# Stick-breaking sums as head and rest products in fp32r, with softplus moved between weight pieces, and differential masks over two blocks

## The reference, cut to what matters

```
z = einsum('bqhd,bkhd->bhqk', qb, k) * scale
log_1m_beta = where(strict, log_sigmoid(-z), 0.0)
suffix = cumsum(log_1m_beta, axis=3, reverse=True) - log_1m_beta
a = where(strict, exp(log_sigmoid(z) + suffix), 0.0)
o = einsum('bhqk,bkhd->bqhd', a, v)
```

## Time and profile before

| | |
|---|---|
| median of 3 runs | 1457.71 us (1454.75 to 1459.5) |
| the profiled execution's own time | 1457.98 us |
| its span, first to last instruction | 1456.3 us |
| PE busy | 1394.3 us (96%), 6857 matmuls |
| weight loads of PE | 1129.3 us (78%) |
| DVE busy | 1004.0 us (69%) |
| ACT busy | 795.2 us (55%) |
| POOL busy | 166.0 us (11%) |
| mean granted TensorE clock | 0.993 |
| chain that ended last | PE 83%, DVE 11%, ACT 2%, issue 2%, DMA 1% |

### The profile page before, as it was taken

The page is one execution under the profiler, slowest core; times in us unless marked ns, Lnnn a source line. Parts: engine busy times, 40 slices in busy tenths (PEclk is TensorE's granted clock), DMA queues, the critical chain, the costliest instruction groups (busy, mean ns, idle before and its releaser), DMA issues.

```text
span 1456.3 us, 20416 instructions
## 1 busy us (share of the span) xinstructions
PE 1394.3 (96%) x6857; PEld 1129.3 (78%) x6857; DVE 1004.0 (69%) x1909; ACT 795.2 (55%) x1560; POOL 166.0 (11%) x315
## 2 busy tenths in 40 slices
PE   7898999998999999998999999999999999999998
PEld 6687788886888788887878888777878888777556
DVE  6887755558655855569667555589777767689876
ACT  6565654546654645456656444466664545575334
POOL 4000000000110100002000000000029992000000
PEclk9999999999999999999999999999999999999999
DMA  8542555554432755564226565444346556443132
GB/s 259 167 145 87 190 200 185 190 179 156 143 116 87 230 181 195 175 195 135 88 72 232 176 198 188 158 161 144 117 137 213 192 173 201 133 157 116 59 105 98
DMA packets 154244, 230.54 MB, mean 158 GB/s; under 512 B 7496, under 2 KB 103056, under 8 KB 154176
## 3 DMA queue, kind: packets, MB, share of 16 engines
q1 hardware_dynamic: 152208, 224.24, 47.1%
q0 software_dynamic: 1968, 5.43, 1.4%
HBM read 228.60 MB, written 1.05 MB: 158 GB/s over the span
## 4 chain that ended last, share of the span: by engine, by line
PE 83%; DVE 11%; ACT 2%; issue 2%; DMA 1%; SPq 0%; DVEq 0%; ACTq 0%
PE ps L1979 24%; PE ps L1981 24%; PE ps L1980 23%; DVE w_rest L1296 3%; PE ps L2746 1%; PE ps L2189 1%; DVE qkv L1420 1%; DVE x L1348 1%; DVE qkv L1418 1%; PE ps L2130 1%; PE ps L2642 1%; ACT scr_a L763 1%; ACT w_head L776 1%; PE ps L2356 1%; DVE tok L1340 0%
## 5 line engine op out<-in xcount | busy, mean ns | idle before, releaser
L1979 PE MATMUL ps<-w_head,xt_head 128*128 128x512 f32 (+1 forms) x1376 | 545.0, 396 | 22.4 <-DVE w_rest L1296 7.8
L1981 PE MATMUL ps<-w_head,xt_rest 128*128 128x512 f32 (+1 forms) x1376 | 530.6, 386 | 0.0
L1980 PE MATMUL ps<-w_rest,xt_head 128*128 128x512 f32 (+1 forms) x1376 | 530.1, 385 | 0.0
L1296 DVE SCALAR_TENSOR_TENSOR w_rest<-w_raw,gain_t,w_head 128x512 fp32r<-128x512 f32 (+1 forms) x600 | 414.3, 754 | 78.0 <-ACT w_head L776 77.2
L776 ACT ACTIVATE w_head<-w_raw,gain_t 128x512 fp32r<-128x512 f32 (+1 forms) x600 | 374.0, 700 | 138.2 <-PE ps L1981 117.9
L1979 PEld LDWEIGHTS ps<-w_head,xt_head 128*128 128x128 f32 x1376 | 260.4, 189 | 84.8 <-DVE xt_rest L1303 17.2
L1981 PEld LDWEIGHTS ps<-w_head,xt_rest 128*128 128x128 f32 x1376 | 259.9, 189 | 53.2
L1980 PEld LDWEIGHTS ps<-w_rest,xt_head 128*128 128x128 f32 x1376 | 260.6, 189 | 46.7
L1294 DVE TENSOR_TENSOR w_rest<-w_raw,w_head 128x1024 fp32r<-128x1024 f32 x124 | 153.8, 1281 | 88.9 <-ACT w_head L776 88.9
L776 ACT ACTIVATE w_head<-w_raw 128x1024 fp32r<-128x1024 f32 x124 | 124.5, 1054 | 105.3 <-PE ps L1981 91.9
L1979 PE MATMUL ps<-w_head,ht_head 128*128 128x512 f32 x320 | 125.0, 391 | 0.3 <-DVE ht_rest L1866 0.3
(11 more groups left out here) (467 smaller groups left out, 1379.8 us busy)
## 6 DMA issues: line engine op xcount, KB each, us to landing
w_raw<-in_ffn_w_gate_dram SPq DMA_DIRECT2D x88, 512.0 KB, 3.9
w_raw<-in_ffn_w_up_dram SPq DMA_DIRECT2D x88, 512.0 KB, 4.9
w_raw<-in_ffn_w_down_dram SPq DMA_DIRECT2D x88, 512.0 KB, 4.2
w_raw<-in_a_w_in_dram SPq DMA_DIRECT2D x48, 512.0 KB, 4.7
w_raw<-in_b_w_in_dram SPq DMA_DIRECT2D x24, 512.0 KB, 4.6
w_raw<-in_w_in_dram SPq DMA_DIRECT2D x24, 512.0 KB, 4.7
w_raw<-in_a_w_out_dram SPq DMA_DIRECT2D x16, 512.0 KB, 4.1
w_raw<-in_c_w_in_dram SPq DMA_DIRECT2D x10, 512.0 KB, 4.4
```

Of the source, the lines that this page charges most:

```text
L1296: ins = dve.scalar_tensor_tensor(w_rest[:, s, w], w_raw[:, s, w], by, hd, ALU.mult, ALU.subtract)
L1979: pe.matmul(out_, hd, wh, start=first, stop=False)
L1980: pe.matmul(out_, hd, wr, start=False, stop=False)
L1981: return pe.matmul(out_, rt, wh, start=False, stop=last)
```

## The change

1. **Suffix sums in fp32r.** After POOL's mask (now `sp_cut`) ACT rounds the two heads' 384 columns each into `spent_head` (`spent_rounded`, the tiles `ht_head` and `ht_rest` of the FFN), DVE subtracts to get `spent_rest` (`spent_rest_of`; tile `share_rest` and a new tile `spent_r`), and `sp_done` comes after that. PE's `suffixes` makes eight fp32r matmuls for a pair (four of 384 columns with the triangle, four of 128 with the ones) in place of six fp32 calls. POOL puts fp32r copies of the two constants into free parts of the same tiles (`signs`). ACT waits for `suf_ready` of the pair before, since there is one `spent_head` for each head.
2. **Softplus between pieces.** `soft_plus(s - 4)` stands on ACT behind the first piece of the unit, `spend(s - 4)` on DVE behind the first piece's rest.
3. **Differential mask.** The mask "diff" goes; the layers use the last 256 columns of "window", and the matmul covers columns 128 to 384.
4. **`share_rest`** is computed in the FFN of layer 1 (`share_split`), from a DMA of its own into `sc`; the fp32r cast at the start has 768 columns, not 1152.

```
@@ tiles
+        spent_head = [flat(t_[:, :, :], MAP) for t_ in (ht_head, ht_rest)]
+        spent_rest = [share_rest, spent_r]
+        neg_tri_r, neg_ones_r = (t_[:, 1, P:2 * P] for t_ in (ht_head, ht_rest))
+        share_raw = sc[:, 0, 0:MAP]
@@ gpsimd
+            def signs(u):
+                pool.wait_ge(unit_used, u)
+                pool.tensor_copy(neg_tri_r, C("neg_tri"))
+                pool.tensor_copy(neg_ones_r, C("neg_ones")).then_inc(signs_there, 1)
+            def share_split():
+                i_ = MAP * MASKS.index("dilated")
+                pool.dma_start(share_raw, a["constants"][:, N_CONST + i_:N_CONST + i_ + MAP]).then_inc(share_in, 16)
+                pool.wait_ge(share_in, 16)
+                pool.tensor_tensor(share_rest[:, :], share_raw, masks_r[:, i_:i_ + MAP].bitcast(F32), ALU.subtract).then_inc(share_there, 1)
...
-            pool.wait_ge(masks_done, 1)
-            i_ = MAP * MASKS.index("dilated")
-            pool.tensor_tensor(share_rest[:, :], masks_raw[:, i_:i_ + MAP], masks_r[:, i_:i_ + MAP].bitcast(F32), ALU.subtract)
...
-                    for there, n_, run, done in ((sp_raw, p_, spent, sp_done), (stick_e, p_ - 1, stick_w, stick_done)):
+                    for there, n_, run, done in ((sp_raw, p_, spent, sp_cut), (stick_e, p_ - 1, stick_w, stick_done)):
@@ scalar, stick
+                def spent_rounded(t):
+                    act.wait_ge(sp_cut, t + 1)
+                    for c in range(2):
+                        act.activation(spent_head[c], spent[t % 2][:, c, :], ACT.Copy).then_inc(sp_head, 1)
...
-                    head(u + s + RING)
+                    head(u + s + RING, between=(lambda: soft_plus(s - 4)) if s >= 4 else None)
...
+                    if s >= 5:
+                        act.wait_ge(suf_ready, s - 4)
                     if s >= 4:
-                        soft_plus(s - 4)
+                        spent_rounded(s - 4)
@@ vector, stick
+                def spent_rest_of(t):
+                    for c in range(2):
+                        dve.wait_ge(sp_head, 2 * t + c + 1)
+                        last = dve.tensor_tensor(spent_rest[c][:, :], spent[t % 2][:, c, :], spent_head[c].bitcast(F32), ALU.subtract)
+                    last.then_inc(sp_done, 1)
...
-                    rest(u + s + RING)
+                    rest(u + s + RING, between=(lambda: spend(s - 4)) if s >= 4 else None)
                     if s >= 4:
-                        spend(s - 4)
+                        spent_rest_of(s - 4)
@@ tensor, diff
-                i_ = MAP * MASKS.index("diff")
-                mask = masks_r[:, i_:i_ + MAP]
+                i_ = MAP * MASKS.index("window")
+                mask = masks_r[:, i_ + P:i_ + MAP]
...
-                        pe.matmul(ps[:, 6 + c, 0:MAP], ident_r[:, :], mask, start=True, stop=False, skip_group_check=True)
+                        pe.matmul(ps[:, 6 + c, P:MAP], ident_r[:, :], mask, start=True, stop=False, skip_group_check=True)
@@ tensor, stick
                 def suffixes(t):
+                    if t == 0:
+                        pe.wait_ge(signs_there, 1)
                     pe.wait_ge(sp_done, t + 1)
                     for c in range(2):
-                        z, run = z_map(t)[:, c, :], spent[t % 2][:, c, :]
-                        pe.matmul(z[:, 0:256], C("neg_tri"), run[:, 0:256], start=False, stop=True, skip_group_check=True)
-                        pe.matmul(z[:, 128:256], C("neg_ones"), run[:, 256:384], start=False, stop=True, skip_group_check=True)
-                        last = pe.matmul(z[:, 256:384], C("neg_tri"), run[:, 256:384], start=False, stop=True, skip_group_check=True)
+                        z = z_map(t)[:, c, :]
+                        for run in (spent_head[c], spent_rest[c]):
+                            pe.matmul(z, neg_tri_r, run[:, 0:MAP], start=False, stop=True, skip_group_check=True)
+                            last = pe.matmul(z[:, P:2 * P], neg_ones_r, run[:, 2 * P:MAP], start=False, stop=True, skip_group_check=True)
```

More of the change, by code:

```diff
@@ L83, in constants @@
         ("odd_group", (i // 16 % 2 == 1).astype(float)),
-        ("diff", np.concatenate([zero, causal, causal], 1)),
         ("window", np.concatenate([np.where(j > i, 0.0, NEG), causal, causal], 1)),
@@ L96 @@
 constants()
-N_CONST = CONSTS["diff"][0]
+N_CONST = CONSTS["window"][0]
 MAP = 384
-MASKS = ("diff", "window", "dilated")
+MASKS = ("window", "dilated")
 MIXER = {
@@ L214, in build @@
         masks_r = sb("masks_r", [P, len(MASKS) * MAP], F32R)
+        spent_r = sb("spent_r", [P, MAP], F32R)
         share_rest = sb("share_rest", [P, MAP], F32R)
@@ L372, in build @@
         sp_raw = sem("sp_raw")
+        sp_cut = sem("sp_cut")
+        sp_head = sem("sp_head")
+        signs_there = sem("signs_there")
+        share_in = sem("share_in")
+        share_there = sem("share_there")
         sp_done = sem("sp_done")
@@ L732, in masks @@
                             last.then_inc(done, 1)
+            u = 0
             for li, kind in enumerate(layer_names):
                 if kind == "stick":
+                    signs(u)
                     masks()
+                u += units_of(kind) + OUT_UNITS + FFN_UNITS
                 for i in (2 * li, 2 * li + 1):
@@ L742, in _ @@
                         s5_loads()
+                        share_split()
                     elif i == 3:
@@ L764, in square, with head @@
                 scratch.append(over)
-            def head(u, more=0):
+            def head(u, more=0, between=None):
                 if isinstance(more, int) and more == 0 and u >= TOTAL:
@@ L774, in head @@
                     act.wait_ge(unit_used, u - RING + 1 + more * RING)
-                for w, by, count in pieces(u):
+                for i, (w, by, count) in enumerate(pieces(u)):
+                    if between and i == 1:
+                        between()
                     ins = act.activation(w_head[:, s, w], w_raw[:, s, w], ACT.Copy, scale=1.0 if by is None else by)
@@ L835, in spread_out @@
                     act.wait_ge(t_ready, n["pair"] + t + 1)
+                    if t == 2:
+                        act.wait_ge(share_there, 1)
                     if t >= 4:
@@ L1282, in step, with rest @@
                 dve.wait_ge(v_step, n["chain"])
-            def rest(u, more=0):
+            def rest(u, more=0, between=None):
                 if isinstance(more, int) and more == 0 and u >= TOTAL:
@@ L2134, in scores @@
                     half = [slice(HD * c, HD * c + HD) for c in range(2)]
+                    if t == 0:
+                        pe.wait_ge(share_there, 1)
                     for c in range(2):
```

## The result

The change made the kernel slower, outside the predicted range: 1465.27 us in the median of 8 executions (1461.14 to 1467.65) against 1455.92 for the kernel before on the same chips (8 executions), ratio 1.0057, 95% interval 1.0045 to 1.007. The profiled execution took 1465.46, its span 1463.7, which is 7.4 more than the 1456.3 of the span before. (One execution of a later run, e1_coef, took 3546.98 us; it is left out of the ratios, and so that kernel has a second run for its profile.)

The account below looks back on a forecast made before the run. PE was taken to set the pace of the steps with pairs, DVE that of the start. +0.15 + 1.7 - 1.4 - 1.2 = -0.75 on 1457.98 us gave 1457.2, or 1457.0 as a median; range 1452.5 to 1461.

Parts of the forecast that it names:

- The clock: Behind PE's 2.4 us idle ahead of maps(6) the clock falls to 1.2 GHz for 3.4 us: +1.7 us.
- The sums: Suffix sums on PE take 1.24 us a pair, saving 0.62, or 5.0 us for eight if PE stays the bound.
- The port: In the stick layer POOL's selects come 0.85 us later beside DVE's rests; the pair's path is 8.0 us.
- Rival 1: In the stick layer the selects get in ahead of the rests; 1452.2 to 1453.9 us, chance 0.2.
- rival 2: In the stick layer the selects wait for the rests, but the clock does not fall; 1455.3 us, chance 0.17.
- rival 4: In the suffix sums fp32r of 128 columns costs as fp32, 0.23 us: +1.8, 1458.8 us; within the forecast's chance 0.5.
- Rival 3: POOL's selects held two whole pieces and more at each pair, path longer than the old step; 1462.7 us, chance 0.13.
- Pair 5: With s5_coefficient behind the subtractions, maps(6) may start 18.05 us after pair 4's maps; PE idles 2.4, 1.5 us lost.
- The other steps of the stick layer: maps(2) 0.6 us late, the last sums' path ending at 8.75 us; all steps of the layer together +0.15 us.
- The start: DVE, the bound up to 48.02 us, loses a subtraction, a third of a cast and waits: -1.4 us, bounds -0.8 and -1.6.
- Differential masks: Mask matmuls in the differential layers, 128 columns less, 0.05 to 0.06 us each: -1.2 us, bounds 0 and -1.8.
- Masks and start together: Shorter mask matmuls in the differential layers, -1.2 us, and less DVE work at the start, -1.4 us: -2.6.

Follow-up runs that it names:

- e1_coef: The changed kernel with s5_coefficient in step 10 instead of step 8; 1455.33 us, ratio to the kernel before 0.9993.
- e6: The kernel before with weights(4) done seven times and the sums of pair 5 behind values(0) to values(3); 1466.03 us, ratio 1.0058.
- e11: The changed kernel with values(0) to values(3) behind the first quarter of unit(11)'s products instead of ahead of them; 1458.1 us, ratio 1.0018.
- e2: The changed kernel with values(0) to values(3) behind three quarters of unit(11)'s products instead of ahead of them; 1458.75 us, ratio 1.0018.
- e8: The changed kernel with s5_coefficient in step 10 and spend behind all pieces of the unit on DVE; 1471.21 us, ratio 1.0098.
- e10: The changed kernel with s5_coefficient in step 10, weights ahead of the roundings on ACT, sums of pair 7 behind values(4); 1452.44 us, ratio 0.9976.
- e7: The kernel before with only the differential mask and share_rest parts of the change; 1455.89 us, ratio 0.9994.
- e3: The kernel before with weights(4) on ACT done seven times instead of once; 1462.69 us, ratio 1.0041.
- e1b: The changed kernel with s5_coefficient in step 10 instead of step 8, run once more for its profile; 1455.88 us, ratio 0.9999.
- e4: The kernel before with weights(4) on ACT done five times instead of once; 1458.1 us, ratio 1.0005.
- e5: The changed kernel with the suffix sums in plain fp32 on spent, as before the change; 1458.16 us, ratio 1.0012.
- e9: The changed kernel with weights(s-5) ahead of spent_rounded(s-4) on ACT; 1455.61 us, ratio 1.001.

## Why the prediction was wrong

**The clock, the step that failed.** "3.4 us of half clock cost 1.7. The idle 2.4 us ahead of maps(6) is as long. +1.7 us." The idle came as predicted (2.44), and so did the fall. Its cost was 8.55. I took the length of the fall from the earlier trace rows, where PE worked on 512-column products behind it, and did not ask what PE works on behind maps(6): 24 calls of 64 columns. They don't bring the clock back (e6), the sums and six products do (e11), and with those the fall costs the 1.7 of the prediction (e2, e11). That 2.4 us of idle are followed by a fall was right at this place, in five profiles of five, but it is no rule: 2.81 us in e8 brought none. This term alone is 6.85 us of an error of 8.3 (1465.46 in the profiled execution, 1457.2 predicted in its terms).

**The sums.** A saving of 0.62 a pair was predicted and about 0.6 measured, but by errors that cancel. The new sums were put at 1.24 (the terms, 0.1 + 4 x 0.28, make 1.22) and took 1.20, while the old ones, read by the start of the next product as these are, took 1.78 and not 1.86. And of the terms, an fp32r matmul of 128 columns costs 0.06 (443.96 to 444.02), the low bound, not the 0.11 chosen, and one of 384 columns in this company 0.23, not 0.17. The Trainium skill ("TensorE: Matmul & The Clock Gate", Back-to-back issue gap) gives, for 128 columns, 81 ns in a stream with weight loads and some 56 alone. The trace has 0.06 here, which fits the second, and 0.11 at half clock (422.07 to 422.18).

**The port.** Right: selects 1.67 behind pieces of 512 and 1.84 behind one of 1024, +0.90 and +1.07 against 0.77, where 0.85 and 1.0 were predicted; 0.77 without rests beside them (e8). The rule of the Trainium skill ("SBUF — State Buffer", Who interferes with whom) agrees with these numbers. Rival 1 is out by the selects, rival 2 by the fall, rival 4 by the 0.06 above. Rival 3, which foresaw a slower kernel, isn't the reason for the slower one: the path of pair 4 was 8.29, the old step, where 8.0 was predicted, and the selects lost 0.90, not two whole pieces.

**Pair 5.** 18.05 predicted from pair 4's maps to maps(6), 420.83 - 402.36 = 18.47 measured; the idle 2.4 and 2.44. e1_coef shows that `s5_coefficient` was its cause.

**The other steps of the stick layer** were each a little worse: maps(2) 0.9 late by a wait of 1.1 (0.6 predicted), the sums of pair 7 at 451.93 - 442.83 = 9.10 behind their maps instead of 8.75. The prediction had left the order weights behind roundings as it was; e10 shows that these waits were what ate most of the sums' gain.

**The start.** -1.4 predicted, -1.0 measured. PE's wait there now ends 0.57 earlier, at 47.45, though DVE's rests ahead of these steps began 0.43 later than before (24.50 against 24.07), so the stretch itself is 1.0 shorter:

```profile
27.20 1.02 DVE L1432 TENSOR_SCALAR ms<-sq 128x2 f32<-128x2 f32 x1
...
28.34 0.16 DVE L1434 TENSOR_SCALAR rs_a<-ms 128x2 int32<-128x2 int32 x1
...
29.90 3.50 DVE L1332 SCALAR_TENSOR_TENSOR w_rest<-w_raw,gain_t,w_head 128x512 fp32r<-128x512 f32 x4
```

The step behind the subtraction fell from 0.99 to 0.16, that behind the cast from 1.35 to 1.02, and a third step, which POOL's next operation had held, from 0.62 to 0.16: the 0.8, 0.35 and 0.4 of the prediction. But the four rests took 3.50, 0.6 more than before (2.89), with POOL's next operations (29.99 to 34.10) beside them, which I had priced at 0.1 to 0.2. That PE was some 1.5 us ahead at 77 us all the same is in part due to the clock: the fall that follows began 0.8 behind the wait's end before (48.86) and begins 1.1 ahead of it now (46.34), so that about 0.55 of what it costs lies inside the wait.

**Differential masks.** -1.2 predicted, and in the trace 0.2 in the first layer and 0.35 in the second. The price of the matmuls was right, that PE sets the pace was not: the two of a pair take 66.17 - 65.76 = 0.41, where they took 67.78 - 67.25 = 0.53, but behind them PE waits longer for DVE's `mix`, 1.12 us behind pair 2's scores where it was 0.86. How the rest of the 0.12 a pair was lost I did not follow.

**Masks and start together** had looked like a sure 2.6 us. The 1.4 to 1.7 us that the trace of e7 shows were not to be seen in its median; falls of the clock at other places of the kernel shifted with them and took as much.

## What to carry to other kernels

Where a change opens an idle stretch of PE, read what PE does in the microseconds behind it: in this kernel products of 512 columns, and calls of 128 and 256 too, brought the clock back soon, a run of 64-column calls did not, and was paid at half clock to its end. Either close the stretch, or put some longer calls between it and the short ones. An instruction that an engine issues while it waits for another (the weights, while ACT waits for POOL's select) cost nothing here, and a small block of scalar work that sits on the critical engine may be moved to where that engine waits anyway.

## What was not expected of the hardware

- Ahead of maps(6) the clock fell at the idle stretch of 2.4 to 2.5 us in each of the five profiles that have one (after, e2, e3, e6, e11), and behind 0.7, 0.8, 1.8 and 1.9 us in none of the profiles of e1b, e4, e5 and e9. It fell 0.1 ahead of the idle's end in e3 and e6, and 1.0 to 1.6 us behind it in the changed kernel, e2 and e11.
- That is no rule for other places. 2.81 us brought no fall in e8. The waits of 1.94 to 2.06 us at 110 us brought one in all thirteen profiles, and the same waits in the second differential layer (near 1040) in twelve; e6 has none there. What decides it isn't shown.
- At full clock, 24 calls of 64 columns in a row leave the clock alone (e11, and the kernel before); at half clock the same calls don't raise it (10.2 us in the changed kernel, 7.6 in e8, and in e6). Full speed came 4.9 us behind the first 512-column product in the changed kernel, 3.7 in e8 and 1.7 in e6, where fp32 sums had run ahead of it.
- An edit of 1 to 2 us shifts which of the short waits elsewhere are followed by a fall of the clock (near 660, 950, 980 and 1045 us), worth up to 3.5 us in the mean of e7: more than the edit.
